# A decoder layer whose gate and up projections take seven block products for eight in more chunk pairs

## The chip, the cores and the metric

One core of a Trainium2 chip runs the whole kernel. The metric is the device time of one execution in microseconds, as the median of several runs.

## The reference, cut to what matters

One decoder layer, 256 tokens, width 2048, everything in fp32. Between the attention and convolution part and a gated input at the end stands a SwiGLU feed-forward with 5632 inner columns:

```
f = rmsnorm(h, g_ffn)
h = h + (silu(f @ w_gate) * (f @ w_up)) @ w_down
```

## The kernel before, in words

Every fp32 matmul is made of three on rounded parts: each operand is split into a high part and the residue, and high x high, high x residue and residue x high are summed in PSUM. ScalarE writes the high part of a weight tile (`split_hi`, L655), VectorE the residue (`split_lo`, L978), from the raw tile that a DMA on SP's queue has brought. SP has four raw buffers.

The feed-forward takes the 5632 columns in 11 panels of 512. Panel 0's gate and up run in a stage of their own ahead of the loop: 16 halves (`gate_and_up`, L1639), `FFN0` to `LOOP0`. Then come ten passes (`feed_forward`), the first written out, eight in a hardware loop, the last written out. A pass computes gate and up of the next panel and then adds the down projection of the panel before. The 16 chunks of 128 rows are taken in eight pairs.

- A plain pair "P" (`eight_products`, L1692) has two units (weight tiles of 1024 columns), eight block products of 128x128 by 512 columns, three matmuls each.
- A seven-product pair "S" (`seven_products`, L1668) treats 2 token blocks x 2 chunks and 2 chunks x (gate, up) as 2x2 matrices and takes seven products, on sums and differences of blocks. Its four units are the two tiles taken as they are (1024 columns), one tile (512 columns), and two tiles of sums (1024 each). The sums of the weights are made by VectorE in every pass (`weight_sums`, L1236: one operation of 1024 columns, then two of 512), the sums of the activation once, ahead of the loop (`x_sums`, L1216; split by `s_hi` and `s_lo`, L1232, by groups of two pairs).
- The down projection has eight units of 12 matmuls each (`add_tokens_by_columns`, L1432).

`QUAD_KINDS` (L72) is the list of the eight pairs. Split tiles go into `LOOP_SLOTS` (L77) slots by turns, so ScalarE and VectorE split a tile that many units ahead; `slot_free` (L357) waits for TensorE's count `half_done`. Each engine's order is written by hand. In a pass VectorE and ScalarE do at step t what is due there, and then split unit t + 8. The seven products add up in the banks P1 to P7; `combine` (L1255) makes the four outputs of them. P1, P5 and P7, P6 serve also as banks of the down projection (`DOWN_BANKS`): `seed` (L831) writes h into them, `read_back` (L844) reads it out (`h_back`).

After pair 0 TensorE turns the activation of the panel before (`turn_act`, L1634, eight transposes) into `ACT_BANKS`; ScalarE and VectorE read the banks (`act_hi` L850, `act_lo` L1197), and the banks can then be written again (`actT_ready`). In `seven_products` the first S pair waits for that at P1 (L1678) and for the read-backs at P7 (L1686).

In the stage before the loop VectorE also normalises the activation (`normalise`, L1204), makes the sums, and writes the residues of the normalised pairs (`a_lo`, L1210). The steps are `NORMAL_AT`, `X_SUMS_AT`, `S_AT` and `A_AT` (L86 to L91): at step m the order is normalise, `x_sums`, `a_lo`, `s_lo`, and then the residue of half m + 4.

Of the kernel before, what the change touches and what calls it, by code (L numbers as in the profile page):

```python
# [68 lines left out]
LOOP0 = FFN0 + 16  # L69
LOOPS = FP - 1  # L70
QUADS = KC // 2
QUAD_KINDS = "PPSSPSSP"  # L72
QUAD_UNITS = [4 if kind == "S" else 2 for kind in QUAD_KINDS]
QUAD_AT = [sum(QUAD_UNITS[:i]) for i in range(QUADS + 1)]
DOWN_AT = QUAD_AT[QUADS]
PER_LOOP = DOWN_AT + 8
LOOP_SLOTS = 8  # L77
S_QUADS = [i for i in range(QUADS) if QUAD_KINDS[i] == "S"]
S_FIRST, S_LAST = S_QUADS[0], S_QUADS[-1]
PLE0 = LOOP0 + PER_LOOP * LOOPS  # L80
# [11 lines left out]
RAW = 4  # L92
# [46 lines left out]
def lo_count(m, it=0):  # L139

    return sum(by_pool(i) == by_pool(m) for i in range(m + 1)) + PER_LOOP * it
# [32 lines left out]
def hybrid_decoder_layer(nc, x, p, g_mix, w_in, w_dw, b_dw, g_conv_ln, b_conv_ln, w_out, g_ffn,  # L174
# [11 lines left out]
    with ExitStack() as ctx:  # L186
# [111 lines left out]

        P1, P5, P2, P3, P4, SPARE, P7, P6 = ps
        DOWN_BANKS = [(P1, P5), (P7, P6), (P1, P5), (P7, P6)]  # L300
        ACT_BANKS = (P1, P5)

        SCORES_BANK, LN_BANK = ps[4], ps[5]

# [21 lines left out]
        def slot_of(m):  # L326

            if LAST <= m < LAST + 4:
                return spare_hi[:, m - LAST], spare_lo[:, m - LAST]
            if in_loop(m):  # L330
                n = (m - LOOP0) % LOOP_SLOTS
                if n == 4:
                    return tuple(o[:, 12:16].rearrange("p (k a) t -> p k (a t)", k=2) for o in (oT_hi, oT_lo))
                if n == 5:
                    return w_more[:, 0:2], w_more[:, 2:4]
                if n >= 6:
                    return w_extra[:, n - 6, 0:2], w_extra[:, n - 6, 2:4]
                return w_hi[:, n], w_lo[:, n]
            return w_hi[:, m % SLOTS], w_lo[:, m % SLOTS]

# [10 lines left out]
        def tiles_of(m):  # L351
# [2 lines left out]
            hi, lo = slot_of(m)  # L354
            return (hi[:, 0:1], lo[:, 0:1]) if one else (hi, lo)

        def slot_free(engine, m, it=0):  # L357

            if LAST <= m < LAST + 4:
                engine.wait_ge(half_done, PG0)  # L360
            elif m >= LAST + 4:
                engine.wait_ge(half_done, m - 2 * SLOTS + 1)
            elif LOOP0 + SLOTS <= m < LOOP0 + LOOP_SLOTS:

                engine.wait_ge(half_done, FFN0)
            elif in_loop(m) and m >= LOOP0 + LOOP_SLOTS:
                engine.wait_ge(half_done, m - LOOP_SLOTS + 1 + PER_LOOP * it)
            elif PLE0 <= m < PLE0 + SLOTS:
                engine.wait_ge(half_done, m - LOOP_SLOTS + 1)
            elif m >= SLOTS:  # L370
                engine.wait_ge(half_done, m - SLOTS + 1)

# [48 lines left out]
        def _(sp):  # L421
# [59 lines left out]
                sp.dma_start(raw[:, 0:4:3], w_gate_v[:, 2 * i:2 * i + 2, cols]).then_inc(quad_ready[i % RAW], 16)  # L481
                sp.dma_start(raw[:, 1:3], w_up_v[:, 2 * i:2 * i + 2, cols]).then_inc(quad_ready[i % RAW], 16)

            def quad_split(i, it):

                sp.wait_ge(lo_ready, lo_count(LOOP0 + QUAD_AT[i] + 1, it))

            def down_split(c, it):
                sp.wait_ge(lo_ready, lo_count(LOOP0 + DOWN_AT + 2 * c + 1, it))
# [10 lines left out]
                load_quad(i, slice(NP, 2 * NP))  # L500
                n += 1

            def feed_forward(it, last):

                for i in range(RAW, QUADS):
                    quad_split(i - RAW, it)
                    load_quad(i, bass.ds(it * NP + NP, NP))
                for c in range(4):
                    quad_split(c + RAW, it)
                    load_down(c, bass.ds(it * 4, 4))  # L510
                if not last:
                    for i in range(RAW):
                        down_split(i, it)
                        load_quad(i, bass.ds(it * NP + 2 * NP, NP))

            feed_forward(0, False)
            with sp.Fori(1, LOOPS - 1) as it:
                feed_forward(it, False)
            feed_forward(LOOPS - 1, True)
# [113 lines left out]
        def _(sc):  # L633
# [241 lines left out]
            for m in range(IN0, LOOP0):  # L875
                step(m)
                if m == LOOP0 - 1:
                    sc.wait_ge(rstd_ready, 3)
                    swish_of(LOOP0)
                for i in range(QUADS):  # L880
                    if m == A_AT[i]:
                        a_hi(i)
                for g in range(len(S_GROUPS)):
                    if m == S_AT[g]:
                        s_hi(g)
                split_hi(m + AHEAD)
            for m in range(LOOP0 + SLOTS, LOOP0 + LOOP_SLOTS):
                if m == LOOP0 + SLOTS + 2:
                    act_hi(ACT_BANKS, 0)
                split_hi(m)  # L890

            def feed_forward(it, last, first=False):

# [78 lines left out]
        def _(ve):  # L972
# [285 lines left out]
            for m in range(IN0, LOOP0):  # L1258
                step(m)
                if m == RB1_AT:  # L1260
                    ve.wait_ge(rb_spread, 2)
                    nc.vector.tensor_copy(rb[:, :], LOW[1][0][:, 0:T]).then_inc(rb2_ready, 1)
                for i in range(QUADS):
                    if m == NORMAL_AT[i]:
                        normalise(i)
                for g in range(len(S_GROUPS)):
                    if m == X_SUMS_AT[g]:
                        x_sums(g)
                if m == LOOP0 - 1:
                    ve.wait_ge(panel_read, Q_DOWN)  # L1270
                    first_swiglu()
                    split_lo(m + AHEAD)
                for i in range(QUADS):
                    if m == A_AT[i]:
                        a_lo(i)
                for g in range(len(S_GROUPS)):
                    if m == S_AT[g]:
                        s_lo(g)
                if not by_pool(m + AHEAD) and m < LOOP0 - 1:
                    split_lo(m + AHEAD)  # L1280
            for m in range(LOOP0 + SLOTS, LOOP0 + LOOP_SLOTS):
                if m == LOOP0 + SLOTS + 2:
                    act_lo(ACT_BANKS, 0)
                if m in (LOOP0 + SLOTS, LOOP0 + SLOTS + 1):
                    weight_sums(m - LOOP0 - SLOTS, 0, S_FIRST)
                split_lo(m)

            def feed_forward(it, last, first=False):

                for t in range(PER_LOOP):  # L1290
# [23 lines left out]
                        ins.then_inc(act_ready, 1)  # L1314
                    for i in S_QUADS:
                        ahead = QUAD_AT[i] - LOOP_SLOTS
                        if ahead >= 0 and t in (ahead, ahead + 1):
                            weight_sums(t - ahead, 0, i, it)
                        if ahead < 0 and not last and t - PER_LOOP in (ahead, ahead + 1):
                            weight_sums(t - PER_LOOP - ahead, 1, i, it)  # L1320
                    m = LOOP0 + t + LOOP_SLOTS
                    if not last or t + LOOP_SLOTS < PER_LOOP:
                        split_lo(m, it)
# [103 lines left out]
        def _(pe):  # L1427
# [237 lines left out]
                hi, lo = slot_of(m)  # L1665
                return hi[:, f], lo[:, f]

            def seven_products(i, it, first_pass):  # L1668

                at = LOOP0 + QUAD_AT[i]  # L1670
                s_hi, s_lo = s_parts(S_QUADS.index(i))
                s1, s2, s3, s4 = ((s_hi[:, 0, k], s_lo[:, 0, k]) for k in range(4))
                first, last = i == S_FIRST, i == S_LAST
                pe.wait_ge(a_ready, i + 1)
                pe.wait_ge(s_ready, S_QUADS.index(i) // 2 + 1)
                arrived(at, it)
                if first:
                    pe.wait_ge(actT_ready, it + 1)  # L1678
                block_product(P1, x_block(i, 0, 0), unit_tile(at, 0), first, last)
                block_product(P2, x_block(i, 0, 1), unit_tile(at, 1), False, False).then_inc(half_done, 1)  # L1680
                arrived(at + 1, it)
                block_product(P3, s4, unit_tile(at + 1, 0), False, False).then_inc(half_done, 1)
                arrived(at + 2, it)
                block_product(P5, s1, unit_tile(at + 2, 0), first, last)
                if first and not first_pass:
                    pe.wait_ge(h_back, 8 * it)  # L1686
                block_product(P7, s3, unit_tile(at + 2, 1), first, last).then_inc(half_done, 1)
                arrived(at + 3, it)
                block_product(P6, s2, unit_tile(at + 3, 0), first, last)
                block_product(P4, x_block(i, 1, 1), unit_tile(at + 3, 1), False, False).then_inc(half_done, 1)  # L1690
# [57 lines left out]
            def feed_forward(it, first_pass=False):  # L1748

                for i in range(QUADS):  # L1750
                    if QUAD_KINDS[i] == "S":
                        seven_products(i, it, first_pass)
                    else:
                        eight_products(i, it, first_pass)
                    if i == 0:
                        if not first_pass:
                            pe.wait_ge(h_back, 8 * it - 2)
                        turn_act(ACT_BANKS, it)
                for c in range(4):
                    pe.wait_ge(h_seeded, 2 * (c + 1) + 8 * it)  # L1760
                    for k in range(2):
                        rows = slice(2 * k, 2 * k + 2)
                        add_tokens_by_columns(LOOP0 + DOWN_AT + 2 * c + k, DOWN_BANKS[c], oT_hi[:, rows], oT_lo[:, rows], k == 1, it)
# [82 lines left out]
```

## Time and profile before

| | |
|---|---|
| median of 3 runs | 1161.87 us (1161.85 to 1162.01) |
| the profiled execution | 1161.71 us, of which the trace spans 1159.9 |
| granted TensorE clock, mean | 0.998 |
| TensorE matmul busy | 1147.7 us, 99% of the span, 5618 instructions |
| TensorE weight load | 968.7 us, 84% |
| VectorE | 899.9 us, 78% |
| ScalarE | 709.7 us, 61% |
| GpSimd | 125.2 us, 11% |
| moved by DMA | 223.38 MB, mean 193 GB/s |

Busy is the time in which an engine has an instruction of its own running; waits, branches and the issuing of DMAs do not count. Matmuls are pipelined: each is shown with 0.39 us, but the next starts before it ends, so for TensorE starts tell more than durations. In the rows PE is TensorE, PEld its weight load, DVE VectorE, ACT ScalarE, SP SyncE; L978 is a line of the kernel. A name of a tile stands without its buffer's number.

### The profile page before, as it was taken

How to read it: one execution, taken by the hardware profiler on the slowest of the kernel's cores; microseconds unless marked ns; L12 is line 12 of the kernel's file. 1: busy time of each engine (PE TensorE's matmuls, PEld its weight loads, DVE VectorE, ACT ScalarE, POOL GpSimd, SP SyncE). 2: the span in 40 equal slices, each digit the busy share in tenths (PEclk: the TensorE clock that was granted, in tenths of full speed). 3: DMA queues.
4: the chain of work that ended last, by engine and by line, in shares of the span. 5: the costliest groups of instructions: out<-in, count | busy, mean ns of one | idle time of the engine just before them, and what ended most of it. 6: DMA issues, size and time to landing. Idle time of an engine off the chain costs nothing.

```text
span 1159.9 us, 16445 instructions
## 1 busy us (share of the span) xinstructions
PE 1147.7 (99%) x5618; PEld 968.7 (84%) x5618; DVE 899.9 (78%) x1192; ACT 709.7 (61%) x969; POOL 125.2 (11%) x74
## 2 busy tenths in 40 slices
PE   9999999999999999999999999999999999999996
PEld 8889989988888878888888888888888888888886
DVE  6589767767777998978888887888787888837674
ACT  6544465466455676766758566667667575757552
POOL 0212443436031000000000000000000000000111
PEclk9999999999999999999999999999999999999999
DMA  9655555454555566564746474755647475754541
GB/s 343 216 183 180 182 182 167 161 179 148 200 167 178 181 240 205 199 225 146 252 146 239 160 252 145 253 176 193 209 157 243 144 252 161 238 212 154 200 160 73
DMA packets 113120, 223.38 MB, mean 193 GB/s; under 512 B 5193, under 2 KB 6417, under 8 KB 112816
## 3 DMA queue, kind: packets, MB, share of 16 engines
q1 hardware_dynamic: 112608, 222.08, 56.8%
q10 hardware_dynamic: 464, 0.66, 0.2%
q8 instruction: 29, 0.48, 0.2%
q14 instruction: 19, 0.16, 0.0%
HBM read 220.63 MB, written 2.10 MB: 192 GB/s over the span
## 4 chain that ended last, share of the span: by engine, by line
PE 92%; DVE 2%; ACT 2%; issue 2%; POOL 1%; POOLq 0%; DVEq 0%; ACTq 0%
PE ps L1655 11%; PE ps L1657 11%; PE ps L1656 11%; PE ps L1452 8%; PE ps L1454 8%; PE ps L1453 8%; PE ps L1439 6%; PE ps L1441 6%; PE ps L1440 6%; PE ps L1486 3%; PE ps L1485 3%; PE ps L1484 3%; PE ps L1494 2%; PE ps L1648 1%; PE ps L1649 1%
## 5 line engine op out<-in xcount | busy, mean ns | idle before, releaser
L655 ACT ACTIVATE w_hi<-w_raw 128x1024 fp32r<-128x1024 f32 (+1 forms) x286 | 290.8, 1026 | 218.0 <-PE ps L1454 120.1
L978 DVE TENSOR_TENSOR w_lo<-w_raw,w_hi 128x1024 fp32r<-128x1024 f32 x250 | 301.4, 1218 | 142.8 <-ACT w_hi L655 142.5
L1452 PE MATMUL ps<-w_hi,nT_hi 128*128 128x512 f32 x280 | 111.4, 398 | 0.0
L1454 PE MATMUL ps<-w_hi,nT_lo 128*128 128x512 f32 x280 | 109.1, 390 | 0.0
L1453 PE MATMUL ps<-w_lo,nT_hi 128*128 128x512 f32 x280 | 109.0, 389 | 0.0
L579 POOL TENSOR_TENSOR w_lo<-w_raw,w_hi 128x1024 fp32r<-128x1024 f32 x36 | 86.7, 2409 | 181.7 <-ACT w_hi L655 181.7
L978 DVE TENSOR_TENSOR w_extra<-w_raw,w_extra 128x1024 fp32r<-128x1024 f32 (+1 forms) x60 | 67.1, 1132 | 37.6 <-ACT w_extra L655 35.4
L1034 DVE SCALAR_TENSOR_TENSOR ps<-arena,taps,ps 128x256 f32<-128x256 f32 x232 | 94.7, 483 | 0.2 <-ACT ps L776 0.2
L1655 PE MATMUL ps<-w_hi,nT_hi 128*128 128x512 f32 x220 | 86.5, 393 | 0.0
L1657 PE MATMUL ps<-w_hi,nT_lo 128*128 128x512 f32 x220 | 85.8, 390 | 0.0
L1656 PE MATMUL ps<-w_lo,nT_hi 128*128 128x512 f32 x220 | 85.6, 389 | 0.0
L573 POOL TENSOR_TENSOR rstd<-msq,power 128x2 f32<-128x2 f32 x4 | 2.8, 708 | 726.9 <-DVE msq L1009 725.6
L655 ACT ACTIVATE w_hi<-arena 128x1024 fp32r<-128x1024 f32 x40 | 42.5, 1062 | 56.8 <-PE ps L1657 36.8
L1484 PE MATMUL ps<-nT_hi,w_hi 128*128 128x256 f32 x256 | 72.9, 285 | 0.0
L1486 PE MATMUL ps<-nT_hi,w_lo 128*128 128x256 f32 x256 | 72.4, 283 | 0.0
L1485 PE MATMUL ps<-nT_lo,w_hi 128*128 128x256 f32 x256 | 72.4, 283 | 0.0
L978 DVE TENSOR_TENSOR w_lo<-arena,w_hi 128x1024 fp32r<-128x1024 f32 x40 | 48.0, 1222 | 27.2 <-ACT w_hi L655 27.2
L1452 PE MATMUL ps<-w_hi,oT_hi 128*128 128x512 f32 x160 | 63.5, 397 | 0.0
L1439 PE MATMUL ps<-w_hi,oT_hi 128*128 128x512 f32 x160 | 62.4, 390 | 0.6 <-ACT ps L842 0.6
L1454 PE MATMUL ps<-w_hi,oT_lo 128*128 128x512 f32 x160 | 62.4, 390 | 0.0
L1453 PE MATMUL ps<-w_lo,oT_hi 128*128 128x512 f32 x160 | 62.3, 389 | 0.0
L842 ACT ACTIVATE ps<-h 128x512 f32<-128x512 f32 x80 | 44.9, 594 | 28.4 <-DVE arena L1256 26.8
(285 smaller groups left out, 2823.6 us busy)
## 6 DMA issues: line engine op xcount, KB each, us to landing
w_raw<-in_w_gate SPq DMA_DIRECT2D x88, 512.0 KB, 4.0
w_raw<-in_w_up SPq DMA_DIRECT2D x88, 512.0 KB, 4.8
w_raw<-in_w_down SPq DMA_DIRECT2D x44, 1024.0 KB, 5.0
w_raw<-in_w_in SPq DMA_DIRECT2D x32, 1024.0 KB, 5.1
w_raw<-in_w_out SPq DMA_DIRECT2D x16, 1024.0 KB, 5.0
w_raw<-in_w_pgate SPq DMA_DIRECT2D x16, 1024.0 KB, 5.0
w_raw<-in_w_in SPq DMA_DIRECT2D x14, 512.0 KB, 10.7
w_raw<-in_w_ple SPq DMA_DIRECT2D x2, 1024.0 KB, 7.0
```

What stands on the lines that cost most here:

```text
L655: nc.scalar.activation(tiles_of(m)[0], source_of(m), ACT.Copy).then_inc(hi_ready, 1)
L978: nc.vector.tensor_tensor(lo, source_of(m), hi.bitcast(F32), ALU.subtract).then_inc(lo_ready, 1)
L1439: nc.tensor.matmul(banks[t][:, :], x_hi[:, k, rows], hi[:, k], start=False, stop=False, skip_group_check=True)
L1452: nc.tensor.matmul(banks[t][:, :], x_hi[:, k, rows], hi[:, k], start=start, stop=False)
L1453: nc.tensor.matmul(banks[t][:, :], x_hi[:, k, rows], lo[:, k], start=False, stop=False)
L1454: ins = nc.tensor.matmul(banks[t][:, :], x_lo[:, k, rows], hi[:, k], start=False, stop=stop)
L1484: nc.tensor.matmul(dst, w_hi[:, s, k, cols], x_hi[:, k], start=start, stop=False, skip_group_check=True)
L1485: nc.tensor.matmul(dst, w_hi[:, s, k, cols], x_lo[:, k], start=False, stop=False, skip_group_check=True)
L1486: ins = nc.tensor.matmul(dst, w_lo[:, s, k, cols], x_hi[:, k], start=False, stop=stop, skip_group_check=True)
L1655: nc.tensor.matmul(bank[:, :], x[0], w[0], start=first, stop=False)
L1656: nc.tensor.matmul(bank[:, :], x[0], w[1], start=False, stop=False)
L1657: return nc.tensor.matmul(bank[:, :], x[1], w[0], start=False, stop=last)
```

## The change

The list of pairs goes from four S pairs to five: pairs 1 to 4 in a row, and pair 6 behind the plain pair 5. A pass has 34 units in place of 32. The sums of the fifth S pair take the part of `oT` that was slot 4, so there are seven slots; as 34 is no multiple of seven, slots are counted from each pass's start (`slot_back`). The activation is turned into P7 and P6, so `turn_act` waits for all read-backs, and the first S pair waits for `actT_ready` at P7, its fourth product. Ahead of the loop, VectorE makes the first sum of weights of the second S pair too, and the split of the normalised pairs 6 and 7 moves behind the splits of units 4 to 6. The groups of activation sums become three: pairs 1 and 2, 3 and 4, and 6.

```diff
-QUAD_KINDS = "PPSSPSSP"
+QUAD_KINDS = "PSSSSPSP"
...
-LOOP_SLOTS = 8
+LOOP_SLOTS = 7
...
-        ACT_BANKS = (P1, P5)
+        ACT_BANKS = (P7, P6)
...
-                n = (m - LOOP0) % LOOP_SLOTS
+                n = (m - LOOP0) % PER_LOOP % LOOP_SLOTS
                 if n == 4:
-                    return tuple(o[:, 12:16].rearrange("p (k a) t -> p k (a t)", k=2) for o in (oT_hi, oT_lo))
-                if n == 5:
                     return w_more[:, 0:2], w_more[:, 2:4]
-                if n >= 6:
-                    return w_extra[:, n - 6, 0:2], w_extra[:, n - 6, 2:4]
+                if n > 4:
+                    return w_extra[:, n - 5, 0:2], w_extra[:, n - 5, 2:4]
...
+        def slot_back(m):
+
+            j = (m - LOOP0) % PER_LOOP
+            if j >= LOOP_SLOTS:
+                return LOOP_SLOTS
+            return PER_LOOP - max(k for k in range(PER_LOOP) if k % LOOP_SLOTS == j) + j
...
-                engine.wait_ge(half_done, m - LOOP_SLOTS + 1 + PER_LOOP * it)
+                engine.wait_ge(half_done, m - slot_back(m) + 1 + PER_LOOP * it)
             elif PLE0 <= m < PLE0 + SLOTS:
-                engine.wait_ge(half_done, m - LOOP_SLOTS + 1)
+                engine.wait_ge(half_done, m - PER_LOOP % LOOP_SLOTS + 1)
...
-            def quad_split(i, it):
-
-                sp.wait_ge(lo_ready, lo_count(LOOP0 + QUAD_AT[i] + 1, it))
+            def quad_split(i, it, first):
+                done = 3 if first and i == S_FIRST else 1
+                sp.wait_ge(lo_ready, lo_count(LOOP0 + QUAD_AT[i] + done, it))
...
-                for i in range(QUADS):
+                for i in range(QUADS - 2):
                     if m == A_AT[i]:
                         a_hi(i)
...
+            for i in (QUADS - 2, QUADS - 1):
+                a_hi(i)
...
-                for i in range(QUADS):
+                for i in range(QUADS - 2):
                     if m == A_AT[i]:
                         a_lo(i)
...
                 split_lo(m)
+            weight_sums(0, 0, S_QUADS[1])
+            for i in (QUADS - 2, QUADS - 1):
+                a_lo(i)
...
-                        if ahead >= 0 and t in (ahead, ahead + 1):
-                            weight_sums(t - ahead, 0, i, it)
-                        if ahead < 0 and not last and t - PER_LOOP in (ahead, ahead + 1):
-                            weight_sums(t - PER_LOOP - ahead, 1, i, it)
+                        for half in range(2):
+                            if t == ahead + half:
+                                weight_sums(half, 0, i, it)
+                            if t - PER_LOOP == ahead + half and not last:
+                                weight_sums(half, 1, i, it)
...
-                if first:
-                    pe.wait_ge(actT_ready, it + 1)
                 block_product(P1, x_block(i, 0, 0), unit_tile(at, 0), first, last)
...
-                if first and not first_pass:
-                    pe.wait_ge(h_back, 8 * it)
+                if first:
+                    pe.wait_ge(actT_ready, it + 1)
                 block_product(P7, s3, unit_tile(at + 2, 1), first, last).then_inc(half_done, 1)
...
-                            pe.wait_ge(h_back, 8 * it - 2)
+                            pe.wait_ge(h_back, 8 * it)
                         turn_act(ACT_BANKS, it)
```

## Rows read from the trace of the kernel before

**Rows 1.** The page, busy time of each engine.

```profile
PE 1147.7 (99%) x5618; PEld 968.7 (84%) x5618; DVE 899.9 (78%) x1192; ACT 709.7 (61%) x969; POOL 125.2 (11%) x74
```

**Rows 2.** Stretches: their length, busy us of each engine, clock, DMA share, GB/s.

```profile
363.30:388.05 24.75, 24.75 (x111) 20.46 (x110) 24.18 (x34) 14.35 (x17) 0.00 (x0) 1.00 0.55 170
...
388.05:454.10 66.05, 64.95 (x285) 52.23 (x284) 59.89 (x67) 45.92 (x60) 0.00 (x0) 1.00 0.64 221
454.10:517.60 63.50, 63.50 (x286) 52.64 (x285) 53.55 (x57) 42.63 (x54) 0.00 (x0) 1.00 0.61 201
```

**Rows 3.** Timeline of TensorE around pair 0 of a pass: start, duration, line.

```profile
644.53 0.39 PE L1655 MATMUL ps<-w_hi,nT_hi 128*128 128x512 f32 x1
...
649.75 0.39 PE L1657 MATMUL ps<-w_hi,nT_lo 128*128 128x512 f32 x1
649.98 1.03 PE L1494 MATMUL ps<-ident,arena 128*128 128x128 f32 x8
...
651.55 0.39 PE L1655 MATMUL ps<-w_hi,nT_hi 128*128 128x512 f32 x1
```

**Rows 4.** Timeline of VectorE: a seven-product pair, the turned activation, a residue.

```profile
604.46 1.23 DVE L1248 TENSOR_TENSOR arena<-w_raw 128x1024 f32<-128x1024 f32 x1
605.60 1.22 DVE L978 TENSOR_TENSOR w_lo<-w_raw,w_hi 128x1024 fp32r<-128x1024 f32 x1
606.74 0.69 DVE L1251 TENSOR_TENSOR arena<-w_raw,arena 128x512 f32<-128x512 f32 x1
607.46 0.69 DVE L1253 TENSOR_TENSOR arena<-w_raw,arena 128x512 f32<-128x512 f32 x1
608.07 0.68 DVE L978 TENSOR_TENSOR w_lo<-w_raw,w_hi 128x512 fp32r<-128x512 f32 x1
608.67 1.22 DVE L978 TENSOR_TENSOR oT_lo<-arena,oT_hi 128x1024 fp32r<-128x1024 f32 x1
...
652.17 1.29 DVE L1200 TENSOR_TENSOR oT_lo<-ps,oT_hi 128x512 fp32r<-128x512 f32 x2 [0.38 <-ACT oT_hi L854]
654.97 1.23 DVE L978 TENSOR_TENSOR w_lo<-arena,w_hi 128x1024 fp32r<-128x1024 f32 x1 [1.51 <-ACT w_hi L655]
```

**Rows 5.** Timeline of ScalarE in the same pass.

```profile
645.70 1.07 ACT L848 ACTIVATE h<-ps 128x512 f32<-128x512 f32 x2
...
650.18 0.63 ACT L655 ACTIVATE w_hi<-w_raw 128x512 fp32r<-128x512 f32 x1 [1.66 <-PE ps L1657]
651.05 1.09 ACT L854 ACTIVATE oT_hi<-ps 128x512 fp32r<-128x512 f32 x2 [0.24 <-PE ps L1494]
653.79 1.06 ACT L655 ACTIVATE w_hi<-arena 128x1024 fp32r<-128x1024 f32 x1 [1.65 <-PE ps L1657]
```

**Rows 6.** Timeline of TensorE: half 13 before the loop, a wait in the first pass.

```profile
379.89 0.39 PE L1648 MATMUL ps<-w_hi,nT_hi 128*128 128x512 f32 x1
...
406.14 0.50 PE L1655 MATMUL ps<-w_hi,oT_hi 128*128 128x512 f32 x1
406.48 0.40 PE L1656 MATMUL ps<-w_lo,oT_hi 128*128 128x512 f32 x1
```

**Rows 7.** Timeline of VectorE in the stage before the loop.

```profile
370.60 1.29 DVE L1208 TENSOR_TENSOR arena<-arena,rb 128x512 f32<-128x512 f32 x2
...
373.54 1.22 DVE L978 TENSOR_TENSOR w_lo<-w_raw,w_hi 128x1024 fp32r<-128x1024 f32 x1
...
375.88 0.41 DVE L1223 TENSOR_TENSOR arena<-arena 128x256 f32<-128x256 f32 x1
...
377.35 0.68 DVE L1214 TENSOR_TENSOR nT_lo<-arena,nT_hi 128x512 fp32r<-128x512 f32 x1
377.95 1.22 DVE L978 TENSOR_TENSOR w_lo<-w_raw,w_hi 128x1024 fp32r<-128x1024 f32 x1
```

**Rows 8.** Timeline of VectorE at the first pass's start.

```profile
389.13 1.41 DVE L1194 SCALAR_TENSOR_TENSOR arena<-ps,rstd,arena 128x512 f32<-128x512 f32 x2 [1.22 <-ACT arena L829]
```

**Rows 9.** The page, DMA issues: size of each, median us from issue to landing.

```profile
w_raw<-in_w_up SPq DMA_DIRECT2D x88, 512.0 KB, 4.8
```

More of the change, by code:

```diff
@@ L501, in _, with feed_forward @@
                 n += 1
-            def feed_forward(it, last):
+            def feed_forward(it, last, first=False):
                 for i in range(RAW, QUADS):
-                    quad_split(i - RAW, it)
+                    quad_split(i - RAW, it, first)
                     load_quad(i, bass.ds(it * NP + NP, NP))
                 for c in range(4):
-                    quad_split(c + RAW, it)
+                    quad_split(c + RAW, it, first)
                     load_down(c, bass.ds(it * 4, 4))
@@ L514, in feed_forward @@
                         load_quad(i, bass.ds(it * NP + 2 * NP, NP))
-            feed_forward(0, False)
+            feed_forward(0, False, True)
             with sp.Fori(1, LOOPS - 1) as it:
@@ L1666, in unit_tile, with seven_products @@
                 return hi[:, f], lo[:, f]
-            def seven_products(i, it, first_pass):
+            def seven_products(i, it):
                 at = LOOP0 + QUAD_AT[i]
@@ L1751, in feed_forward @@
                     if QUAD_KINDS[i] == "S":
-                        seven_products(i, it, first_pass)
+                        seven_products(i, it)
                     else:
```

## The prediction

> **What bounds the kernel now.** I read the page's busy shares first: TensorE is busy for 99% of the span [rows 1]. A busy share does not prove a bound, so I went to the busy times by stretch [rows 2]. A middle pass of the feed-forward loop lasts 63.5 us; TensorE is busy in all of it, VectorE in 53.55, ScalarE in 42.63, at a granted clock of 1.00. The second half of the stage before the loop (363.3 to 388.05) is different: TensorE 24.75 of 24.75, but VectorE 24.18 too. Two engines are full there. The first pass takes 66.05, of which TensorE has 64.95.
>
> TensorE's timeline says what busy means in the loop [rows 3]. Pair 0 starts at 644.53, its 24th matmul at 649.75 and the transposes at 649.98: 5.45/24 = 0.227 us from start to start. From the transposes to the next even beat (three matmuls later, 651.55) is 1.57, so the eight transposes cost 1.57 - 3 x 0.227 = 0.89. One pass is 60 block products of 3 matmuls and 8 halves of 12: 276 x 0.227 + 0.89 = 63.5, the pass itself. Nothing waits in a steady pass, and a matmul less is 0.227 us less there, if VectorE delivers in time.
>
> **The change, part by part.**
>
> *Matmuls.* One plain pair (24 matmuls) becomes a seven-product pair (21) in each of ten passes: 3 x 0.227 = 0.68 us a pass, 6.8 in all. On TensorE nothing else changes in number.
>
> *VectorE in a pass.* A seven-product pair costs it, start to start [rows 4]: difference of two tiles 1.14, residue of unit 0 1.14, two more sums 0.72 + 0.61, residue of unit 1 0.60, residues of units 2 and 3 2 x 1.14: 6.5 us. TensorE takes 21 x 0.227 = 4.76 for the same pair. A plain pair costs VectorE 2 x 1.14 = 2.3 and TensorE 5.45. So VectorE gets 4.2 us more per pass, 53.55 to about 57.7 of 62.8: it still fits on average, but four seven-product pairs in a row cost it 4 x (6.5 - 4.76) = 7 us of its lead. Where is that lead, and what if it is not there? Three places.
>
> *A steady pass* (times from the start of pair 0). The activation must be turned after pair 0, and the pair right behind needs a bank of it (P7) at its fourth product. TensorE is there at 5.45 + 0.89 + 12 x 0.227 = 9.06. Before, a whole pair lay between. ScalarE starts the split behind pair 0 at 5.65 (650.18 - 644.53) [rows 5]; it is now a tile of 1024 columns (unit 8) in place of 512, and the read of the turned banks follows at about 6.6. VectorE: ScalarE's split ends at 5.65 + 1.06, 0.12 later (653.79 + 1.06 to 654.97) [rows 4, 5] the residue starts at 6.83, and the activation's residues, 1.29 for two, run from 7.97 to 9.26. TensorE so waits 0.2 to 0.3, and the first matmul after a wait is followed after 0.34 instead of 0.227 [rows 6]: 0.37 in all. Bounds: nothing (a plain beat saved anywhere hides it) and 0.8 (VectorE one 512-column operation late). I take 0.37, as all its links are rows. Behind it VectorE has no more idle time until the run ends; walking on with 6.5 a pair, its residues for units 2 of the fourth pair are ready at 22.2, and TensorE wants them at 23.0. So the run holds, by 0.8 us. Gain of a steady pass: 0.68 - 0.37 = 0.31, times nine: **-2.8**.
>
> *The stage before the loop.* The groups of sums of the activation go from two (of two pairs) to three (2, 2, 1). VectorE's order for halves 12 and 13 changes. Before [rows 7]: two normalised pairs from 370.60, residue of half 12 at 373.54, the last two normalised, four sums 375.88 to 377.35, a residue 0.60, half 13's residue at 377.95, ready at 379.18; TensorE wants it at 379.89 [rows 6]. After, the sums of pairs 3 and 4 (1.5) come ahead of half 12, which moves to 375.1 and still is in time (wanted at 377.2). Then normalise 1.2, the sums of the single pair, a residue 0.60, the second group's residue (1024 columns, 1.14), and only then half 13. The single pair's four sums have 128 columns; no row has that form. From 512 columns (0.60) to 256 (0.34; four in 1.47 with their waits) [rows 7] the step is 0.26, so 128 is estimated at 0.2, with waits 1.0 for four; the ends are 0 and 1.5. Half 13's residue then starts at 375.1 + 1.14 + 1.3 + 1.0 + 0.6 + 1.14 = 380.3 and is ready at 381.55: TensorE waits 1.7, with the slow start 1.8 (0.8 to 2.3). Half 14 is late by less than TensorE. **+1.8**.
> For that one form the Trainium skill has a price ("VectorE: DVE Perf Modes", the section on the TRN2 errata): an fp32 two-tensor operation of N columns takes (N + 151)/0.96 ns, 0.29 us at 128, an estimate; it gives 0.42 at 256, and this trace has 0.41 [rows 7]. By it the term would stay the same within 0.1.
>
> *The first pass* (times from its first product, 388.05 before [rows 2]). No earlier pass has filled the slots. Before, VectorE starts the first product of gate and up at 1.08 [rows 8], and two plain pairs (11.8 us with the transposes) cover what follows. Now one pair does. VectorE: product 1.08 to 2.4; residue of unit 3, 2.4; difference 3.0 to 4.2; ScalarE splits unit 4 from 4.3 to 5.4; residue 5.5; the two further sums 6.7 to 8.1; ScalarE splits unit 5 8.2 to 9.2; residue 9.4; activation's residues 10.5 to 11.8. TensorE wants them at 9.06 and goes on at 11.9: **2.8** lost. VectorE goes on without a pause: unit 6 11.7, difference for the next pair 12.8, the two residues of the normalised input that the change put here 14.0, two sums 15.2, unit 7 16.5 to 17.2 (wanted at 15.4), unit 8 to 18.3. From there two pairs at 6.5 each: units 10 to 17 end at 32.4, unit 16 at 31.3. TensorE closes the fourth pair two units later, at 34.1; unhindered it would at 5.45 + 0.89 + 4 x 4.76 = 25.4. The pass loses 8.7 and is 62.8 + 8.7 = 71.5 against 66.05: **+5.4**. Its own waits of before (2.6, a seed and late units) go under. Ends: +3.4, if ScalarE and VectorE hand over without the two pauses of 1.3 at units 4 and 5, and +7, if the waits of before come on top.
>
> *Edits at nothing.* Seven slots in place of eight: with 34 units a slot is used again seven units on, at the pass's edge six; the residues there have several halves of 2.7 us in front. The turn waits for all four read-backs; the last ends at 645.70 + 1.07 [rows 5], 2.2 after the pass's start, now about 1 us later, the turn is at 5.45. The queue of SP: each load is released by a residue well ahead of its use, in the tightest place (the third panel of the down projection) by some 6 us, and a landing takes 4.8 [rows 9]; the release that moved (first pass, pair 1) has 15 us.
>
> **Sum:** 1.8 + 5.4 - 2.8 = +4.4, on the profiled execution's 1161.71, which is 0.16 below the median of the runs: 1166.3 on the median.
>
> **The rivals.** (a) *VectorE keeps ahead in the first pass as in a steady one.* It then loses no more than 2.6, as now, and the ten passes give 6.8 less: 1161.9 - 6.8 + 1.8 = 1156.9. Against it: the order of the queue, with two handovers inside, is fixed in the program. It decides whether the activation's residues end before 9.06 in that pass. (b) *Only the wait for the activation fails to show in steady passes*: 9 x 0.37 = 3.3 better, 1163.0, no change. For it: the lateness is only 0.2 to 0.3. (c) *VectorE does not hold the run of four in each pass*: its reserve of 0.8 rests on starts 1.14 apart; one further us in each of nine passes gives 1175. Against it: in a steady pass VectorE's chains ran at these beats without a gap [rows 4]. (d) *The seven-product pairs in the looped passes are not those of the list*: then nothing moves, 1161.9; the loop's bounds are read from the list, so hardly.
>
> **How the numbers follow.** Forecast 0.62, (a) 0.10, (b) 0.15, (c) 0.12, (d) 0.01. A measurement here can tell 0.2% from no change, 2.3 us. Faster is (a): 0.10; within is (b), (d) and the low end of the forecast: 0.18; slower the rest: 0.72. The range leaves out (a) and (c): from 1161.8 ((b) with the stage at its low end) to 1169.8 (first pass and stage at their high ends, with a little more wait per pass).
>
> **What would show it.** Right: steady passes of 63.1 to 63.3 with one gap of 0.2 to 0.3 at the fourth product behind the transposes, released by the activation's residue; a first pass near 71 with gaps of 2.8, 1.9 and then some of 0.3 to 0.6, all released by VectorE; a gap of 1.7 some 8 us before the loop. Wrong: no such gaps in the first pass (a), or gaps on the third and fourth pair in every pass (c).

## The result and the profile after

The changed kernel takes 1166.45 us (median of 5 runs, 1166.0 to 1166.61) against 1161.87 before (1161.8 to 1162.32): ratio 1.0038, 95% interval 1.0026 to 1.005. It is slower by 4.6 us, though it does 30 matmuls fewer.

The page's busy times, which answer to [rows 1]:

```profile
PE 1147.2 (99%) x5588; PEld 963.8 (83%) x5588; DVE 939.9 (81%) x1247; ACT 717.2 (62%) x990; POOL 125.2 (11%) x74
```

The share of TensorE is 99% again, and its busy time 0.5 us less; the page alone hides the change. VectorE has 40 us more. The stretches show where the time is; the columns are as in [rows 2]. The first pass is cut as there; the second runs from its transposes to the next ones (turn to turn); the third is a few us inside the first pass:

```profile
389.79:461.42 71.63, 66.94 (x282) 52.50 (x281) 63.04 (x70) 45.94 (x60) 0.00 (x0) 0.98 0.59 197
466.87:530.10 63.23, 63.11 (x282) 51.99 (x281) 56.32 (x62) 43.17 (x56) 0.00 (x0) 1.00 0.58 200
...
402.30:405.70 3.40, 3.40 (x10) 2.58 (x9) 3.37 (x6) 1.06 (x1) 0.00 (x0) 0.52 0.64 244
```

The first pass takes 71.63, where it took 66.05: 5.6 more. A steady pass takes 63.2; turn to turn over eight passes (466.87 to 972.30) it is 63.18, where the same cut of the kernel before (459.55 to 967.31) gives 63.47. VectorE is at 56.3 of it, ScalarE hardly above before. And in the first pass there is something new, 3.4 us at a granted clock of 0.52.

TensorE's timeline shows each wait as a gap between starts. First half 13 of the stage before the loop, which was at 379.89 without a gap [rows 6]; then the product behind the transposes that needs a bank of the turned activation (P7), in the first pass; then the same place in a steady pass. In the code that is the fifth product, behind P1, P2, P3 and P5, and not the fourth, as the part ahead of the prediction calls it; the prediction's sum has the 12 matmuls of four products ahead of it, so its times are those of the fifth:

```profile
379.96 0.39 PE L1661 MATMUL ps<-w_hi,nT_lo 128*128 128x512 f32 x1
381.46 0.50 PE L1659 MATMUL ps<-w_hi,nT_hi 128*128 128x512 f32 x1 [1.11 <-DVE w_lo L985]
381.81 0.40 PE L1660 MATMUL ps<-w_lo,nT_hi 128*128 128x512 f32 x1
...
398.62 0.39 PE L1668 MATMUL ps<-w_more,oT_lo 128*128 128x512 f32 x1
401.31 0.50 PE L1666 MATMUL ps<-w_more,oT_hi 128*128 128x512 f32 x1 [2.29 <-DVE oT_lo L1207]
401.64 0.40 PE L1667 MATMUL ps<-w_more,oT_hi 128*128 128x512 f32 x1
...
402.66 0.63 PE L1668 MATMUL ps<-w_extra,oT_lo 128*128 128x512 f32 x1
403.08 0.63 PE L1666 MATMUL ps<-w_extra,nT_hi 128*128 128x512 f32 x1
...
406.23 0.40 PE L1668 MATMUL ps<-w_extra,nT_lo 128*128 128x512 f32 x1
406.71 0.50 PE L1666 MATMUL ps<-w_hi,oT_hi 128*128 128x512 f32 x1
...
533.49 0.39 PE L1668 MATMUL ps<-w_more,oT_lo 128*128 128x512 f32 x1
533.96 0.50 PE L1666 MATMUL ps<-w_more,oT_hi 128*128 128x512 f32 x1
534.30 0.39 PE L1667 MATMUL ps<-w_more,oT_hi 128*128 128x512 f32 x1
```

A start comes 0.227 after the one before; what goes beyond is a wait, and 0.11 more follows it (0.34 to the next). So half 13 loses 1.50 - 0.23 + 0.11 = 1.4, the first pass's wait is 2.5, the steady one 0.24, with the slow start 0.35. From 402.66 on the matmuls come 0.43 apart, at the lower of the clock's two levels, and up to speed again only behind 405.64.

VectorE's timeline, first at half 13, then through the first pass, names what is late:

```profile
377.52 0.29 DVE L1230 TENSOR_TENSOR arena<-arena 128x128 f32<-128x128 f32 x1
...
378.46 0.68 DVE L1221 TENSOR_TENSOR nT_lo<-arena,nT_hi 128x512 fp32r<-128x512 f32 x1
379.06 1.22 DVE L1241 TENSOR_TENSOR oT_lo<-arena,oT_hi 128x1024 fp32r<-128x1024 f32 x1
380.19 1.22 DVE L985 TENSOR_TENSOR w_lo<-w_raw,w_hi 128x1024 fp32r<-128x1024 f32 x1
...
395.15 1.22 DVE L985 TENSOR_TENSOR w_more<-arena,w_more 128x1024 fp32r<-128x1024 f32 x1 [1.13 <-ACT w_more L660]
...
398.83 1.23 DVE L985 TENSOR_TENSOR w_extra<-arena,w_extra 128x1024 fp32r<-128x1024 f32 x1 [1.13 <-ACT w_extra L660]
399.97 1.28 DVE L1207 TENSOR_TENSOR oT_lo<-ps,oT_hi 128x512 fp32r<-128x512 f32 x2
...
409.03 1.23 DVE L1255 TENSOR_TENSOR arena<-w_raw 128x1024 f32<-128x1024 f32 x1
...
415.70 1.23 DVE L1255 TENSOR_TENSOR arena<-w_raw 128x1024 f32<-128x1024 f32 x1
```

Half 13's residue stands behind the second group's residue (L1241) and is ready at 381.41, 0.05 before TensorE goes on. The activation's residues (L1207) end at 401.25, 0.06 before. Between the pairs' first operations there are 415.70 - 409.03 = 6.7 us; TensorE would need 4.76.

The account, on the profiles: stage before the loop 1.4, first pass 5.6, nine passes 9 x (63.18 - 63.47) = -2.6, and 0.3 before the stage, where nothing was changed: 4.7, and the spans differ by 4.6. The 0.3 is no effect of the change: the last transposes ahead of the stage stand at 357.65 before and 357.95 after, and between 357.35 and 358.18 over the nine kernels profiled here.

### The profile page after: what moved, and what is told of

Its sections match the earlier page's. It is cut to its first block, busy times and chain, and to the rows that moved or that the text cites. A ratio compares the mean times of both kernels' runs of the same rounds, so it can differ in the third digit from the quotient of the medians.

```text
span 1164.5 us, 16557 instructions
## 1 busy us (share of the span) xinstructions
PE 1147.2 (99%) x5588; PEld 963.8 (83%) x5588; DVE 939.9 (81%) x1247; ACT 717.2 (62%) x990; POOL 125.2 (11%) x74
## 3 DMA queue, kind: packets, MB, share of 16 engines
q1 hardware_dynamic: 112608, 222.08, 56.4%
## 4 chain that ended last, share of the span: by engine, by line
PE 84%; DVE 7%; issue 4%; ACT 3%; POOL 1%; DVEq 0%; ACTq 0%; POOLq 0%
PE ps L1666 9%; PE ps L1667 9%; PE ps L1668 9%; PE ps L1463 8%; PE ps L1465 8%; PE ps L1464 8%; PE ps L1452 6%; PE ps L1450 6%; PE ps L1451 6%; PE ps L1497 3%; PE ps L1496 3%; PE ps L1495 3%; DVE w_lo L985 2%; DVE w_extra L985 1%; DVE oT_lo L1207 1%
## 5 line engine op out<-in xcount | busy, mean ns | idle before, releaser
L660 ACT ACTIVATE w_hi<-w_raw 128x1024 fp32r<-128x1024 f32 (+1 forms) x306 | 302.1, 998 | 206.2 <-PE ps L1465 121.7
L985 DVE TENSOR_TENSOR w_lo<-w_raw,w_hi 128x1024 fp32r<-128x1024 f32 (+1 forms) x270 | 315.9, 1178 | 136.1 <-ACT w_hi L660 135.6
L660 ACT ACTIVATE w_hi<-arena 128x1024 fp32r<-128x1024 f32 x60 | 63.7, 1062 | 85.0 <-DVE arena L1255 36.0
L1463 PE MATMUL ps<-w_hi,nT_hi 128*128 128x512 f32 x280 | 111.4, 398 | 0.0
L1465 PE MATMUL ps<-w_hi,nT_lo 128*128 128x512 f32 x280 | 109.1, 390 | 0.0
L1464 PE MATMUL ps<-w_lo,nT_hi 128*128 128x512 f32 x280 | 109.0, 389 | 0.0
L985 DVE TENSOR_TENSOR w_extra<-w_raw,w_extra 128x1024 fp32r<-128x1024 f32 x60 | 72.2, 1218 | 0.0
L985 DVE TENSOR_TENSOR w_lo<-arena,w_hi 128x1024 fp32r<-128x1024 f32 x60 | 71.3, 1218 | 0.0
L1666 PE MATMUL ps<-w_hi,nT_hi 128*128 128x512 f32 x170 | 67.2, 395 | 1.4 <-DVE w_lo L985 1.4
L1668 PE MATMUL ps<-w_hi,nT_lo 128*128 128x512 f32 x170 | 66.3, 390 | 0.0
L1667 PE MATMUL ps<-w_lo,nT_hi 128*128 128x512 f32 x170 | 66.2, 389 | 0.0
L1463 PE MATMUL ps<-w_hi,oT_hi 128*128 128x512 f32 x160 | 63.5, 397 | 0.0
L1255 DVE TENSOR_TENSOR arena<-w_raw 128x1024 f32<-128x1024 f32 x50 | 61.1, 1222 | 1.9
```

The lines of the kernel that those rows point to most:

```text
L660: nc.scalar.activation(tiles_of(m)[0], source_of(m), ACT.Copy).then_inc(hi_ready, 1)
L985: nc.vector.tensor_tensor(lo, source_of(m), hi.bitcast(F32), ALU.subtract).then_inc(lo_ready, 1)
L1463: nc.tensor.matmul(banks[t][:, :], x_hi[:, k, rows], hi[:, k], start=start, stop=False)
L1464: nc.tensor.matmul(banks[t][:, :], x_hi[:, k, rows], lo[:, k], start=False, stop=False)
L1465: ins = nc.tensor.matmul(banks[t][:, :], x_lo[:, k, rows], hi[:, k], start=False, stop=stop)
L1666: nc.tensor.matmul(bank[:, :], x[0], w[0], start=first, stop=False)
```

## The experiments

Every run is the changed kernel with the edits shown; times are medians, and the ratios stand against the kernel before, measured beside them: 1162.03 for the list alone, the opposite edit and all four edits together, 1161.84 for the others. The changed kernel's 1166.45 was measured beside 1161.87, so differences of 0.2 us from it are within the noise.

**The wait for the activation in a steady pass.** In `feed_forward` of ScalarE and of VectorE:

```diff
-                    if t == 2 and not first:
+                    if t == 1 and not first:
```

> The changed kernel, but in the looped passes and the last one ScalarE and VectorE read the turned activation ahead of the split of unit 8, not behind it. Theory of the prediction (VectorE has a reserve of only 0.8 us in the run of four): the gap of 0.25 at the fourth product behind the transposes goes, but the residue of unit 8 and all behind it come 0.9 later, so the wait reappears at the third unit of the fourth pair (0.3 to 0.6, released by VectorE); steady passes 63.2 to 63.4, the time 1166 to 1169. Rival (that wait is the whole loss of a steady pass): steady passes 62.8, the time 1163.2.

Measured: 1169.79, ratio 1.0069 (1.0055 to 1.0082), 3.3 slower than the change. The gap behind the transposes is gone, and a bigger one stands at the fourth pair. TensorE's timeline of a steady pass, third unit of pair 4:

```profile
547.33 0.40 PE L1668 MATMUL ps<-w_hi,oT_lo 128*128 128x512 f32 x1
547.90 0.50 PE L1666 MATMUL ps<-w_hi,oT_hi 128*128 128x512 f32 x1 [0.17 <-DVE w_lo L985]
548.23 0.39 PE L1667 MATMUL ps<-w_lo,oT_hi 128*128 128x512 f32 x1
```

The second unit waits too (0.34 from start to start). VectorE's timeline ahead of that, from the activation's residues on:

```profile
532.24 1.29 DVE L1207 TENSOR_TENSOR oT_lo<-ps,oT_hi 128x512 fp32r<-128x512 f32 x2 [0.73 <-ACT oT_hi L859]
...
535.82 1.23 DVE L1255 TENSOR_TENSOR arena<-w_raw 128x1024 f32<-128x1024 f32 x1
```

Both engines in the changed kernel, at the same places:

```profile
535.07 1.22 DVE L1255 TENSOR_TENSOR arena<-w_raw 128x1024 f32<-128x1024 f32 x1
...
545.88 2.35 DVE L985 TENSOR_TENSOR w_lo<-arena,w_hi 128x1024 fp32r<-128x1024 f32 x2
...
547.70 0.39 PE L1666 MATMUL ps<-w_hi,oT_hi 128*128 128x512 f32 x1
```

With the reading ahead, VectorE pauses 0.73 for ScalarE's read of the turned banks, and stands 0.8 later behind the transposes: 535.82 - 530.04, where the changed kernel has 535.07 - 530.10. In the changed kernel the residue of the third unit of pair 4 is ready at 545.88 + 1.22 = 547.10 and TensorE takes it at 547.70, a reserve of 0.6. With the reading ahead it is ready at 547.84, and TensorE, which no longer waits behind the transposes, could take it at 547.56. A steady pass takes 63.56, above the 63.2 to 63.4 expected, and the time is above 1169: VectorE's pair is 6.6 here (its first operations stand at 535.82 and 542.42), not the 6.5 of the prediction. In the kernel before, the pair ahead of the one in [rows 4] had 604.46 - 597.87 = 6.59 as well:

```profile
597.87 1.22 DVE L1248 TENSOR_TENSOR arena<-w_raw 128x1024 f32<-128x1024 f32 x1
```

The direction is settled: the small wait in the changed kernel is not the whole loss; the run of four has little reserve behind it, and reading ahead uses that up.

**The run of four.** The same edit with the list `"PSSPSSSP"`:

> The activation read ahead as in the run e1_act_ahead, and five seven-product pairs as a run of two and a run of three (pairs 1, 2 and 4, 5, 6). Theory (the run of four is what the steady pass lacks reserve for): the steady passes have no gap but the transposes, 62.8; first pass about 71.0; the time 3.8 below that of the change, 1162.6. Rival (it is VectorE's 4 us more per pass, wherever they stand): gaps in the second run of each pass, steady passes 63.1 or more, the time 1166.

Measured: 1162.39, ratio 1.0004 (0.9995 to 1.0013). A steady pass has no gap left, by the stretches (from turn to turn):

```profile
466.07:528.95 62.88, 62.88 (x283) 52.01 (x282) 56.40 (x62) 43.02 (x56) 0.00 (x0) 1.00 0.60 201
```

VectorE does as much as in the change (56.4), and a plain pair between the runs gives it time to catch up. So in a steady pass its 4 us more cost nothing as such; where they stand costs. The list alone:

> Only the list is other than in the change: runs of two and of three pairs, the activation read behind the split of unit 8 as in the change. Theory (a steady pass loses to the wait for the activation first, and the run of four only would come next): the gap of 0.25 behind the transposes stays, steady passes 63.2 as in the change, first pass 70.5 as in e4_two_three_ahead, the time 1 less than the change's, 1165.4. Rival (the run of four itself is what costs in the change): steady passes 62.9, the time 1162.4 as there.

Measured: 1165.31, ratio 1.0028 (1.0018 to 1.0039); a steady pass has 63.2 with the same gap (0.48 from start to start, at 532.11 to 532.59) and the first pass 70.56. Both edits together save 1166.45 - 1162.39 = 4.1; the list alone 1.1, the reading ahead alone costs 3.3. They are two limits of one pass, the second just behind the first.

**The size of that wait.** The opposite edit, `t == 3`:

> The changed kernel with ScalarE and VectorE reading the turned activation one unit later still, behind the splits of units 8 and 9, in the looped passes. Theory: TensorE waits 2.5 at the fourth product of each pass in place of 0.25; VectorE is not late behind it, so steady passes are 65.4 if the clock stays up and up to 67 if the granted clock falls behind each such wait as it did in the changed kernel's first pass (0.52 over 3.4 us): 1187 or 1201. Rival (the wait is hidden by work that VectorE would make TensorE wait for anyway): steady passes 64 at most, 1174.

Measured: 1191.79, ratio 1.026 (1.0245 to 1.0276), neither 1187 nor 1201. Each of the nine passes behind the first has the same gap of 2.7 from start to start, but the granted clock falls behind only three of them. The stretches, three neighbouring passes and a few us behind the wait of the third:

```profile
466.77:533.80 67.03, 64.71 (x282) 53.18 (x281) 56.50 (x62) 43.73 (x56) 0.00 (x0) 0.97 0.55 189
533.80:599.21 65.41, 63.07 (x282) 51.99 (x281) 56.27 (x62) 43.73 (x56) 0.00 (x0) 1.00 0.57 192
599.21:666.25 67.04, 64.72 (x282) 53.16 (x281) 56.45 (x62) 43.73 (x56) 0.00 (x0) 0.97 0.55 188
...
607.00:610.30 3.30, 3.30 (x10) 2.56 (x9) 3.25 (x5) 1.06 (x1) 0.00 (x0) 0.50 0.00 0
```

Five passes of 65.4 and three of 67.0 (the last one, which ends otherwise, is 2.24 longer as well): 6 x 2.24 + 3 x 3.85 above the change's 63.18 is 25.0, and 1166.45 + 25.0 = 1191.5. The wait is paid in full here, where VectorE is not late behind it (65.4 against 62.87 without a wait), and a fall of the clock costs 1.6 more.

**The stage before the loop.** The second and third group of sums later:

```diff
-X_SUMS_AT = [NORMAL_AT[group[-1]] for group in S_GROUPS]
-S_AT = [NORMAL_AT[group[-1]] + 1 for group in S_GROUPS]
+X_SUMS_AT = [NORMAL_AT[S_GROUPS[0][-1]], FFN0 + 10, FFN0 + 11]
+S_AT = [X_SUMS_AT[0] + 1, FFN0 + 11, FFN0 + 12]
```

> The changed kernel with the second and third group of activation sums (and their residues) two to three halves later in the stage before the loop. Theory (VectorE's queue was late for half 13 only because the sums came all at once): the gap of 1.5 at half 13 goes and comes nowhere else, first pass and steady passes as they were, the time 1.4 less, 1165.0. Rival (VectorE's total work ahead of the loop is the bound): the gap moves to a later half or into the first pass, the time stays at 1166.4.

Measured: 1164.70, ratio 1.0024 (1.0015 to 1.0034), 1.75 less than the change, 0.3 more than the gap was worth. The gap at half 13 is gone and none comes in its place; the first pass (71.64) and the steady ones (63.2) are those of the change. VectorE's timeline shows half 13's residue (376.06) ahead of the second group's sums, and half 14's (379.26) ahead of the third group's:

```profile
376.06 1.22 DVE L985 TENSOR_TENSOR w_lo<-w_raw,w_hi 128x1024 fp32r<-128x1024 f32 x1
377.19 0.41 DVE L1230 TENSOR_TENSOR arena<-arena 128x256 f32<-128x256 f32 x1
...
379.26 1.22 DVE L985 TENSOR_TENSOR w_lo<-w_raw,w_hi 128x1024 fp32r<-128x1024 f32 x1
380.39 0.28 DVE L1230 TENSOR_TENSOR arena<-arena 128x128 f32<-128x128 f32 x1
```

**The first pass.** VectorE's two pauses filled (ScalarE in step with it: `a_hi` ahead of unit 4, `act_hi` ahead of unit 5):

```diff
-                if m == LOOP0 + SLOTS + 2:
-                    act_lo(ACT_BANKS, 0)
                 if m in (LOOP0 + SLOTS, LOOP0 + SLOTS + 1):
                     weight_sums(m - LOOP0 - SLOTS, 0, S_FIRST)
+                if m == LOOP0 + SLOTS:
+                    for i in (QUADS - 2, QUADS - 1):
+                        a_lo(i)
+                if m == LOOP0 + SLOTS + 1:
+                    act_lo(ACT_BANKS, 0)
                 split_lo(m)
             weight_sums(0, 0, S_QUADS[1])
-            for i in (QUADS - 2, QUADS - 1):
-                a_lo(i)
```

> The changed kernel with another order at the first pass's start: VectorE writes the residues of the normalised pairs 6 and 7 while ScalarE splits unit 4, and the activation's residues while ScalarE splits unit 5, so that its two pauses of 1.1 are filled. Theory (the first pass is bound by VectorE's whole queue up to the fourth pair): the gap of 2.7 goes, but gaps of 0.3 to 1.5 released by VectorE stay in pairs 1 to 4, first pass 69.3 in place of 71.6, the time 2.3 less, 1164.1. Rival (the first pass's loss hangs on the wait for the activation, and on the stretch at half clock behind it): first pass 67, the time 4.5 less, 1162.

Measured: 1163.83, ratio 1.0017 (1.0008 to 1.0026), 2.6 less than the change; the first pass takes 69.36. The gap of 2.7 is gone and the clock stays up in that pass (1.00), but the next gap has grown. TensorE's timeline at the second unit of pair 2:

```profile
402.64 0.39 PE L1669 MATMUL ps<-w_extra,nT_lo 128*128 128x512 f32 x1
404.33 0.50 PE L1667 MATMUL ps<-w_hi,oT_hi 128*128 128x512 f32 x1 [1.30 <-DVE w_lo L985]
```

In the changed kernel the same place has 0.48 (406.23 to 406.71): the slow clock had brought TensorE there late enough. Another trace shows the same pass without the fall. In the run that reads the activation ahead, only the later passes were edited; its first pass has the long wait too, but its granted clock stays at 1.00. The stretch of that pass, and TensorE's timeline:

```profile
389.42:461.04 71.62, 65.39 (x282) 51.38 (x281) 63.02 (x70) 45.94 (x60) 0.00 (x0) 1.00 0.58 197
...
398.28 0.39 PE L1668 MATMUL ps<-w_more,oT_lo 128*128 128x512 f32 x1
400.92 0.50 PE L1666 MATMUL ps<-w_more,oT_hi 128*128 128x512 f32 x1 [2.26 <-DVE oT_lo L1207]
...
404.25 0.39 PE L1668 MATMUL ps<-w_extra,nT_lo 128*128 128x512 f32 x1
406.32 0.50 PE L1666 MATMUL ps<-w_hi,oT_hi 128*128 128x512 f32 x1 [1.69 <-DVE w_lo L985]
```

The pass takes 71.62, as in the changed kernel (71.63), and the second gap is 2.07. So the long wait and the clock's fall cost the first pass nothing of their own; VectorE's queue up to the fourth pair sets its end. Filling the two pauses of 1.13 shortens that queue by 2.26, and the pass by 71.63 - 69.36 = 2.27.

**All four edits together.**

> All four edits together: runs of two and three, the activation read ahead, the late activation sums, the first pass's other order. Theory (four waits in separate places, each in VectorE's queue): the savings add up, gap at half 13 gone, first pass 68 to 69, steady passes 62.9, the time 1162.4 - 1.7 - 2.4 = 1158.3, 0.3% below the kernel before. Rival (one debt of VectorE that is paid somewhere in the first pass): first pass 70 or more, the time 1161 to 1162.

Measured: 1158.68, ratio 0.997 (0.9959 to 0.9981): 7.8 below the change and 3.4 below the kernel before. The stretches, first pass and a steady one:

```profile
388.57:456.88 68.31, 65.40 (x282) 51.32 (x281) 64.09 (x72) 46.01 (x60) 0.00 (x0) 1.00 0.61 208
462.33:525.19 62.86, 62.86 (x282) 52.00 (x281) 56.41 (x62) 43.06 (x56) 0.00 (x0) 1.00 0.59 201
```

The savings add up within 1 us (4.1 + 1.75 + 2.6 = 8.4 against 7.8). The first pass is still 68.3 - 62.9 = 5.4 us longer than a steady one; every wait in it for which the trace names a releaser is on a residue of VectorE.

## Why the prediction was right

- **The sum** (1.8 + 5.4 - 2.8 = 4.4) was measured as 1.4 + 5.6 - 2.6 on the profile, and 4.6 on the medians. That the sum comes within 0.2 is in part luck: the loss in the stage was put 0.4 too high, that in the first pass 0.2 too low, and the gain of the steady passes 0.2 too high. The edits bear out the causes: the stage's term went with the late sums; the steady term went with reading ahead and another list together, not with either alone; of the first pass's loss, filling the pauses took 2.3, and its rest has not been taken away by any run.
- **A matmul less is 0.227 less** held: without the wait a steady pass is 62.87, 0.6 below 63.47, where 0.68 was expected; where the other 0.08 goes is open.
- **The wait for the activation** was there, at the place that the prediction's sum gives and of the size (0.24 of 0.2 to 0.3; with the slow start 0.35 of 0.37).
- **The reserve of the run of four** was put at 0.8 us. In the changed kernel it is 0.6 (547.10 to 547.70), and VectorE standing 0.8 later uses it up and costs 0.7 a pass (63.56 against 62.87). So the term was mis-sized: VectorE needs 6.6 to 6.7 for a pair in a run, not 6.5. The code lets the first difference of a pair wait for the last residue of the pair ahead (`weight_sums`, `lo_ready`), and it starts 1.25 behind that residue's start in a steady pass, 1.33 in the first, not 1.14. The trace of before had this already (6.59), in the pair ahead of the one that was summed. Rival (c) was that near.
- **VectorE's load of a pass**, 57.7 in the prediction, is 56.3: the 53.55 it was added to belongs to a pass cut that held one operation more; the others have 52.5, and 52.5 + 4.2 = 56.7.
- **The stage before the loop**: the place, half 13, was right, the term mis-sized (1.8 for 1.4): the residue was ready 0.4 earlier than walked (381.41 less the 0.3 by which this trace starts later, against 381.55). The four 128-column sums took 0.94 from the first to the next operation, 1.0 was estimated; one of them is 0.28 to 0.29. The estimate by the Trainium skill ("VectorE: DVE Perf Modes", "The TRN2 errata") was 0.29, and the trace agrees.
- **The first pass**: 71.6 of 71.5. Its first wait was 2.5, not 2.8, as the two pauses were 1.13 each, not 1.3. The second, 1.9, did not show in the changed kernel: the clock's fall, which the prediction did not have, stood there in its place. Where the clock did not fall (the first pass of the run that reads ahead) it was 1.84, a gap of 2.07. That the pass comes out within 0.1 is in part luck: the two pauses were 0.3 shorter than walked, and the two pairs behind them 0.2 longer each (6.67 against 6.5). The prediction's low end, +3.4 without the pauses, was measured as 69.36 - 66.05 = 3.3.
- The rivals fell: VectorE does not keep ahead in the first pass (a), the steady wait shows (b), the changed kernel has no gap on the third and fourth pair of a steady pass (c), and the looped passes are each 0.29 shorter (d).

Not tried: a first pass with fewer seven-product pairs than the others. How much of the 5.4 us left this would win is open.

## What to carry to other kernels

A saving on the busiest engine can be paid for by the engine that feeds it, as here; compare the two stage by stage and run by run (6.6 us of VectorE against 4.8 of TensorE in each seven-product pair), since an average over the pass (56 of 63) hides that four in a row eat the lead. The stage in which both engines were full, and the first pass of the loop, had no lead to give: look at such places first. And before a small wait is taken away, walk the queue behind it: here it stood in front of a larger one, and the order of the pairs had to change with it.

## What was not expected of the hardware

The granted clock fell behind waits of 2.5 us, not during them. In the first pass of the changed kernel TensorE starts again at 401.31 at full speed, goes over to 0.43 between starts at about 402.5, and is back at 405.7, 3.4 us at 0.52. The Trainium skill ("TensorE: Matmul & The Clock Gate", "Why this matters for your kernels") warns of idle gaps between bursts of matmuls; the length that it gives is above the 2.5 us (2.69 from start to start) that was enough here, and the measurement decides. It was not always enough: the same pause in nine passes of one run brought the clock down three times, at a cost of 1.6 us each, and in the first pass of the run that reads ahead (2.64 from start to start) the clock stayed up. What decides it is open. In the first pass, where the feeding engine is late behind the wait anyway, the fall cost nothing (71.63 with it, 71.62 without); in the steady passes, without such cover, it was paid for.
